# Second block's mixers: two jobs run earlier, output products spread over the last four steps, output units in another order

## What is computed

```python
def token_mixer(h, w_in, f_bias, cmp_pos, cmp_w1, cmp_w2, w_out, cos, sin):
    proj = h @ w_in
    ...
    o_nsa = nsa_mixer(apply_rope(heads(parts['nsa_q'], NSA_HEADS), cos, sin), ...)
    o_fox = fox_mixer(heads(parts['fox_q'], FOX_HEADS), ..., parts['fox_f'], f_bias)
    o_moba = moba_mixer(apply_rope(heads(parts['moba_q'], MOBA_HEADS), cos, sin), ...)
    return jnp.concatenate([o_nsa, o_fox, o_moba], axis=-1) @ w_out
```

## Time and profile before

| what | us |
|---|---|
| runs of the kernel | 1490.35, 1493.84, 1501.74 (median 1493.84) |
| the profiled execution | 1497.93 |
| its span, first to last instruction | 1496.1 |
| TensorE busy | 1454.9 (97% of the span) |
| VectorE busy | 1149.2 (77%) |
| ScalarE busy | 784.7 (52%) |
| DMA engines, mean share | 57.6% by the main queue |
| granted TensorE clock, mean | 0.989 |

### The profile page before, as it was taken

The page is one execution under the profiler, slowest core; times in us unless marked ns, Lnnn a source line. Parts: engine busy times, 40 slices in busy tenths (PEclk is TensorE's granted clock), DMA queues, the critical chain, the costliest instruction groups (busy, mean ns, idle before and its releaser), DMA issues. The chain is left out here.

```text
span 1496.1 us, 20923 instructions
## 1 busy us (share of the span) xinstructions
PE 1454.9 (97%) x8376; PEld 1250.0 (84%) x8376; DVE 1149.2 (77%) x1607; ACT 784.7 (52%) x1115; POOL 26.3 (2%) x31
## 2 busy tenths in 40 slices
PE   8997999999999999999999999999999999999997
PEld 6885888998788888788798888888888787888886
DVE  6797778898779877676678987789877675787653
ACT  7546555764555534656465542655535564565541
POOL 0021000000000000000000000000000000000000
PEclk9999999999999999999999999999999998999999
DMA  8123377988468787433357769478686341466550
...
DMA packets 57152, 327.19 MB, mean 219 GB/s; under 512 B 6608, under 2 KB 7120, under 8 KB 27600
## 3 DMA queue, kind: packets, MB, share of 16 engines
q1 hardware_dynamic: 55440, 322.76, 57.6%
...
## 5 line engine op out<-in xcount | busy, mean ns | idle before, releaser
L335 DVE TENSOR_TENSOR wlo<-raw,whi 128x2048 fp32r<-128x2048 f32 (+2 forms) x236 | 533.5, 2264 | 88.3 <-ACT whi L328 87.3
L328 ACT ACTIVATE whi<-raw 128x2048 fp32r<-128x2048 f32 (+2 forms) x236 | 445.9, 1895 | 133.9 <-PE ps L1603 98.2
L1356 PE MATMUL ps<-hreg_r,whi 128*128 128x512 f32 x1504 | 359.4, 391 | 0.7 <-DVE mix L1539 0.4
L1356 PEld LDWEIGHTS ps<-hreg_r,whi 128*128 128x128 f32 x1504 | 276.6, 188 | 54.8 <-DVE mix L1539 0.6
L370 DVE CUSTOM_DVE_ANT_0 adaw<-adaw,crow,colp 128x1024 f32<-128x1024 f32 x144 | 182.9, 1280 | 37.8 <-DMA adaw<-in_wada 37.6
L1365 PEld LDWEIGHTS ps<-hreg_r,wlo 128*128 128x128 f32 x1504 | 192.6, 191 | 7.0
L1365 PE MATMUL ps<-hreg_r,wlo 128*128 128x256 f32 x1504 | 195.6, 283 | 0.0
L1533 ACT ACTIVATE mix<-ps 128x512 f32<-128x512 f32 x93 | 55.6, 598 | 219.5 <-PE ps L1365 214.1
L1595 PE MATMUL ps<-whi,ireg_r 128*128 128x512 f32 x416 | 130.3, 394 | 3.5 <-ACT ireg_r L1490 3.5
L1599 PE MATMUL ps<-wlo,ireg_r 128*128 128x512 f32 x416 | 128.7, 391 | 0.0
L1603 PE MATMUL ps<-whi,ireg_r 128*128 128x512 f32 x416 | 128.5, 390 | 0.0
(11 more groups left out here) (415 smaller groups left out, 1883.6 us busy)
## 6 DMA issues: line engine op xcount, KB each, us to landing
...
```

Of the source, the lines that this page charges most:

```text
L328: act.activation(self.whi[:, m, 0:width], self.raw[:, n % NRAW, 0:width], ACT.Copy).then_inc(*self.A.done("hi", n))
L335: dve.tensor_tensor(self.wlo[:, m, 0:width], self.raw[:, n % NRAW, 0:width], self.whi[:, m, 0:width].bitcast(F32), ALU.subtract).then_inc( ...
L1356: pe.matmul(self.ps[:, b, :], self.whi[:, m, c:c + 128], self.hboth[:, kt], start=kt == 0, stop=False)
```

## The change

`JOBS` gives each position p the job that runs there: fox's jobs 8 and 9 come fifth and sixth, 4 to 7 seventh to tenth. Semaphores are now named by position. In step order:

- Both pairs of D's heads are turned in step 3 (before, one in step 3 and one in step 4); projection E's second half is copied by ScalarE instead of VectorE.
- The mixed slices kt 4 and 5 (fox) and 6 and 7 (moba) are turned in pairs for all 256 tokens (`turn_pair`, `mixed_pair`), the first pair in step 8. `out` takes parts: six matmuls with kt 4 and 5 stand ahead of `values(8)` and of `values(10)`, and the slices 0 to 3 of tokens 0 follow in the last step, one product on each side of `values(11)`.
- The two compressed products follow each other in step 10; E's heads are turned behind `values(8)`.
- On ScalarE `hidden(0)` and `hidden(1)` stand ahead of the splits that they followed, and the splits of the output units come one place earlier or more. On VectorE the split of unit n0+16 stands ahead of the compressed keys' copies, the next one follows at once, the rope stands behind `maxima(9)`, and `emit` of jobs 4 to 7 releases by its third operation.
- The output units are used and loaded in the order (0, 0), (0, 1), (512, 1), (512, 0) of columns and half.

The diff, cut to its core; the rest renames g to p and defines `turn_pair`, `mixed_pair` and `paired_cols`:

```diff
@@ -58,6 +58,7 @@
 
 
 SPARSE = range(4, 12)
+JOBS = [0, 1, 2, 3, 8, 9, 4, 5, 6, 7, 10, 11]
 
 
 def slot_of(e):
...
-        order.extend([(("w_out2", l), c, h, UW) for h in range(2) for c in (0, 512)])
+        order.extend([(("w_out2", l), c, h, UW) for c, h in ((0, 0), (0, 1), (512, 1), (512, 0))])
         ffn(l, 1)
     return order
 
...
@@ -2377,33 +2384,27 @@
                 mm = pe.matmul(o, self.ahi[:, kv, kt, :], wl, start=False, stop=kt == 15)
             mm.then_inc(*P.done("unit", n))
...
 
-        def out(c, kts, t, free=None):
-
-            if free is not None:
-                pe.wait_ge(*free)
+        def out(c, kts, t, start=False, stop=False):
+
             bank, tk = ps[:, 6 * (1 - t) + c, :], slice(128 * t, 128 * t + 128)
+            n = UNIT[("w_out2", l), 512 * c, kts[0] // 4]
+            m = n % NSPL
+            if t == 0:
+                pe.wait_ge(*A("hi", n))
             for kt in kts:
-                n, i = UNIT[("w_out2", l), 512 * c, kt // 4], kt % 4
-                m = n % NSPL
-                wh = self.whi[:, m, 512 * i:512 * i + 512]
-                if i == 0:
-                    pe.wait_ge(*A("hhi", (st, "o"), kt, t))
-                    pe.wait_ge(*V("hlo", (st, "o"), kt, t))
-                if t == 0 and i == 0:
-                    pe.wait_ge(*A("hi", n))
-                pe.matmul(bank, self.hhi[:, kt, tk], wh, start=kt == 0, stop=False)
+                wh = self.whi[:, m, 512 * (kt % 4):512 * (kt % 4) + 512]
+                pe.matmul(bank, self.hhi[:, kt, tk], wh, start=start and kt == kts[0], stop=False)
                 pe.matmul(bank, self.hlo[:, kt, tk], wh, start=False, stop=False)
             if t == 0:
                 pe.wait_ge(*V("lo", n))
             for kt in kts:
-                i = kt % 4
-                wl = self.wlo[:, m, 512 * i:512 * i + 512]
-                mm = pe.matmul(bank, self.hhi[:, kt, tk], wl, start=False, stop=kt == 7)
+                wl = self.wlo[:, m, 512 * (kt % 4):512 * (kt % 4) + 512]
+                mm = pe.matmul(bank, self.hhi[:, kt, tk], wl, start=False, stop=stop and kt == kts[-1])
             if t == 1:
                 mm.then_inc(*P.done("unit", n))
-            elif kts[-1] == 7:
+                P.at["pj", (st, "o"), c, 1] = P.n
+            elif stop:
                 mm.then_inc(*P.done("pj", (st, "o"), c, 0))
-            P.at["pj", (st, "o"), c, 1] = P.n
 
...
             tr.then_inc(*P.done("zz", st, kv))
 
-        def turn_mix(a, z, t, b):
-            for k in range(a, z):
-                tr = pe.transpose(banks4(b)[:, k - a], self.mix[:, t, 128 * k:128 * k + 128], ident)
-            tr.then_inc(*P.done("mT", st, a, t))
-
-        def scores(g):
-            r = g % 2
-            if g >= 2:
-                pe.wait_ge(*A("pc", st, g - 2))
-                pe.wait_ge(*V("pc", st, g - 2))
...
@@ -2538,18 +2545,19 @@
         scores(3)
         chunk("F", 0, 1, V("pj", st, "D"))
         turned_probs(2)
-        chunk("F", 1, 0)
-        values(2)
         pe.wait_ge(*V("zz", st, 1))
         turn_heads("D", 0)
+        chunk("F", 1, 0)
+        pe.wait_ge(*V("turn", st, "D", 0))
+        turn_heads("D", 1)
+        values(2)
 
         scores(4)
         chunk("F", 1, 1)
         turned_probs(3)
         compress(0, 0, A("pj", st, "F"))
         values(3)
-        pe.wait_ge(*V("turn", st, "D", 0))
-        turn_heads("D", 1)
+        pe.wait_ge(*A("turn", st, "D", 1))
 
         scores(5)
         compress(0, 1)
@@ -2562,7 +2570,6 @@
         turned_probs(5)
         chunk("E", 0, 0, A("hg", st, 0))
         values(5)
-        pe.wait_ge(*A("turn", st, "D", 1))
         pe.wait_ge(*A("hg", st, 1))
         for kv in range(2):
             for k in range(2):
@@ -2594,60 +2601,73 @@
         scores(8)
         chunk("E", 1, 1)
         turned_probs(7)
+        pe.wait_ge(*A("pj", st, "E"))
+        pe.wait_ge(*V("em", st, 5))
+        turn_pair(4, 6)
         values(7)
-
 
         scores(9)
         turned_probs(8)
-        pe.wait_ge(*V("rope", st, 2332))
-        pe.wait_ge(*V("Sc", st))
-        turn_heads("E", 0)
+        pe.wait_ge(*A("hhi", (st, "o"), 4))
+        pe.wait_ge(*V("hlo", (st, "o"), 4))
+        out(0, (4, 5), 0, start=True)
         values(8)
-
-        def compressed(t):
-            pe.matmul(ps[:, 5, :], v["PC"][:, t, :], v["VC"].rearrange("p h d -> p (h d)"), start=True, stop=True)\
-                .then_inc(*P.done("oc", st, t))
-
-        pe.wait_ge(*V("turn", st, "E", 0))
-        scores(10)
-        turn_heads("E", 1)
-        turned_probs(9)
-        pe.wait_ge(*A("turn", st, "E", 1))
         pe.wait_ge(*V("cp", st))
         for t in range(2):
             tr = pe.transpose(ps[:, 5, 128 * t:128 * t + 128], v["Sc"][:, t].rearrange("p g j c -> p (g j c)"), ident)
         tr.then_inc(*P.done("PC", st))
+        pe.wait_ge(*V("rope", st, 2332))
+        for k in range(2):
+            for t in range(2):
+                c = MIXC["E"][0] + 256 * k + 128
+                tr = pe.transpose(banks4(7)[:, 2 * k + t], pj[:, t, c:c + 128], ident)
+        tr.then_inc(*P.done("turn", st, "E", 1))
+        pe.wait_ge(*A("PC", st))
+        turn_heads("E", 0)
+
+        def compressed(t, b):
+            pe.matmul(ps[:, b, :], v["PC"][:, t, :], v["VC"].rearrange("p h d -> p (h d)"), start=True, stop=True)\
+                .then_inc(*P.done("oc", st, t))
+
+        pe.wait_ge(*V("turn", st, "E", 0))
+        scores(10)
+        turned_probs(9)
+        compressed(0, 5)
+        pe.wait_ge(*A("turn", st, "E", 1))
+        compressed(1, 7)
         values(9)
-        pe.wait_ge(*A("PC", st))
-        compressed(0)
 
         scores(11)
+        pe.wait_ge(*V("em", st, 9))
+        pe.wait_ge(*V("oc", st, 1))
+        turn_first(0)
         turned_probs(10)
-        pe.wait_ge(*V("oc", st, 0))
-        compressed(1)
+        out(1, (4, 5), 0, start=True)
         values(10)
-        pe.wait_ge(*V("oc", st, 1))
-        turn_mix(0, 4, 0, 5)
-        turn_mix(0, 4, 1, 0)
+
         turned_probs(11)
-
-
-        out(0, range(4), 0, A("pj", st, "E"))
+        pe.wait_ge(*A("hhi", (st, "o"), 0, 0))
+        pe.wait_ge(*V("hlo", (st, "o"), 0, 0))
+        out(0, range(4), 0)
+        turn_first(1)
         values(11)
-        out(1, range(4), 0, V("pj", st, "E"))
+        pe.wait_ge(*A("hhi", (st, "o"), 0, 1))
+        pe.wait_ge(*V("hlo", (st, "o"), 0, 1))
+        out(1, range(4), 0)
         pe.wait_ge(*V("em", st, 11))
-        turn_mix(4, 8, 0, 5)
-        turn_mix(4, 8, 1, 2)
-        out(0, range(4), 1)
+        turn_pair(6, 2)
+        out(0, range(4), 1, start=True)
+        pe.wait_ge(*A("hhi", (st, "o"), 6))
+        pe.wait_ge(*V("hlo", (st, "o"), 6))
         for c in range(2):
-            out(c, range(4, 8), 0)
-        out(1, range(4), 1)
-        out(0, range(4, 8), 1)
+            out(c, (6, 7), 0, stop=True)
+        out(0, range(4, 8), 1, stop=True)
+        out(1, range(4, 8), 1, start=True)
         self.norm_pe(pe, AFTER[st], 0)
-        out(1, range(4, 8), 1)
+        out(1, range(4), 1, stop=True)
 
     def mixer_sp(self, sp, l):
-        for n in range(UNIT[("w_in2", l), "A", 0], UNIT[("w_out2", l), 512, 1] + 1):
+        for n in range(UNIT[("w_in2", l), "A", 0], UNIT[("w_out2", l), 512, 0] + 1):
             self.ada_sp(sp, n)
             self.loads_at(sp, n)
 
...
@@ -2731,6 +2756,7 @@
         exps(3)
         probs(2)
         self.ahead_act(act, n0 + 8)
+        turned("D", 1, 5)
         act.wait_ge(*V("A", st))
         act.activation(self.ahi, v["A"], ACT.Copy).then_inc(*A.done("Ah", st))
         chunk("F", 6)
@@ -2740,46 +2766,47 @@
         self.ahead_act(act, n0 + 9)
 
         exps(5)
-        turned("D", 1)
         probs(4)
+        hidden(0)
         self.ahead_act(act, n0 + 10)
-        hidden(0)
         self.ahead_act(act, n0 + 11)
 
         exps(6)
         probs(5)
+        hidden(1)
         self.ahead_act(act, n0 + 12)
-        hidden(1)
 
         exps(7)
         probs(6)
         self.ahead_act(act, n0 + 13)
         chunk("E", 6)
+        self.ahead_act(act, n0 + 14)
 
         exps(8)
+        probs(7)
         act.wait_ge(*V("cm", st))
         act.activation(v["S16"], v["S16"], ACT.Exp, scale=0.125).then_inc(*A.done("ce", st))
-        probs(7)
-        self.ahead_act(act, n0 + 14)
+        act.wait_ge(*P("pj", st, "E", 1))
+        act.activation(pj[:, 1, 2332:2844], ps[:, 7, :], ACT.Copy).then_inc(*A.done("pj", st, "E", 1))
+        mixed_pair(4, 6)
 
         probs(8)
         exps(9)
-
-        turned("E", 1)
-        probs(9)
+        self.ahead_act(act, n0 + 15)
         act.wait_ge(*P("PC", st))
         act.activation(v["PC"].rearrange("p t c -> p (t c)"), ps[:, 5, 0:256], ACT.Copy).then_inc(*A.done("PC", st))
+        turned("E", 1, 7)
+
+        probs(9)
         exps(10)
 
+        mixed(0)
         probs(10)
         exps(11)
-        mixed(0, 4, 0, 5)
-        mixed(0, 4, 1, 0)
+        self.ahead_act(act, n0 + 16)
```

(55 more changed lines are left out.)

128 lines of the change are left out of this document (77 added, 51 removed).

## The result

The change made the kernel slower: 1519.11 us, median of four executions (1512.33 to 1524.26), against 1497.26 us for the kernel before, run beside it. The ratio is 1.0129, with a 95% interval of 1.0096 to 1.0162. A second run of the same pair gave 1.0126 (1.0106 to 1.0146): 1517.8 against 1497.5 us by the medians, and 19.3 us more by the means. The forecast was 1505.5 us with a range that ended at 1513, so the size was missed. The ratios are estimated over executions and aren't the quotients of the medians: the two differ by up to 0.2% (1.0129 and 1.0146 in the first run).

The account below looks back on a forecast made before the run. TensorE bounds the mixers, losing time to idling and ungranted clock. Per mixer, 8.4 us new waits less 2.85 removed is +5.55; two mixers +11.1, clock +0.8, on 1493.84 make 1505.7, say 1505.5 us; range 1493 to 1513.

Parts of the forecast that it names:

- `compress(1,1)`: Step 6: the compressor product waits for a split now behind the GELU on ScalarE, 0.9 us a mixer (0.5 to 1.1).
- compressed keys: Compressed scores wait for copies now behind VectorE's split of unit n0+16, 0.65 us a mixer (0.3 to 1.0).
- `values(8)`: Values wait for `emit(7)`, now behind the rope on VectorE: 2.9 us a mixer (2.6 to 3.3) where 1.25 stood.
- E's heads: `scores(10)` waits for the copy of E's turned heads, now turned behind `values(8)`: 0.9 us a mixer (0.7 to 1.2).
- `values(9)`: Values wait for VectorE's split, maxima, probabilities and `emit(8)`: 1.2 us a mixer (0.8 to 1.5).
- small ones: PC's copy behind a split, `emit(9)` ahead of `turn_first(0)`, lower half ahead of the second output product: 0.6 us a mixer.
- into the next stage: Norm behind the mixer: TensorE waits for the diagonal and then the turned tiles, 1.25 us a mixer (0.5 to 2).
- the clock's term: Both mixers: five or six stretches of 3.41 us at half clock in all where five were, +0.8 us.
- the second fall of the kernel before: Clock fall in step 8, said to have no fox in front but a 1.25 us wait; used against regained clock.
- rival C: Clock lost: fox's rows in steps 4 and 5 and the 2.9 us wait add two low stretches a mixer; 1512 us, chance 0.18.
- B: Clock regained in both mixers, waits as worked out: -7.9 us of clock, 1497 us, chance 0.12.
- D: Output matmuls cover `emit(7)` and clock is regained; new waits under 6.8 us a mixer, 1486 us were they 3; chance 0.15.

Follow-up runs that it names:

- the filled wait: Changed kernel with 12 unread matmuls of 512 columns put into TensorE's wait ahead of `values(8)`: 1514.5 us; with the bias rows widened too, 1512.7 us.
- fox128: Fox's bias rows contracted over 128 rows (127 of them zeros) instead of one: changed kernel 1513.7 us; kernel before, ratio 0.9980 and 0.9983.
- the emits first: Kernel before with VectorE's `emit(6)` to `emit(9)` ahead of the maxima and probabilities that stood in front: ratio 0.9968.
- the kernel before with two short waits: Kernel before with `hidden(0)` ahead of ScalarE's split and VectorE's split ahead of the compressed keys' copies: ratio 1.0043.
- the mended places: Changed kernel with VectorE's and ScalarE's order turned in four places: 1498.5 us, 1.0001; `emit(7)` first alone 1.0053, other three 1.0029, two of these 1.0044.

## Why the prediction was wrong

**The waits were right, one by one.** For a mixer, forecast and measured at full clock in the list of waits: `compress(1,1)` 0.9 and 0.91; compressed keys 0.65 and 0.94; `values(8)` 2.9 and 2.8; E's heads 0.9 and 0.85; `values(9)` 1.2 and 1.21, visible in the two kernels with the filled wait; small ones 0.6 and 0.2; into the next stage 1.25 and, at the norm's line, 0.79 and 0.74. The measured ones sum to 8.4 us, as the forecast ones did. Less the 2.85 us that were removed it is 5.55 us a mixer, 11.1 us in all. The mixers' length less 1.2 each says 9.0 us (310.5 less 301.5), and the norms behind them took 2.3 us more: 11.3 us by another way, as far as the net price of 1.2 holds. In the profile of the kernel after itself the wait ahead of `values(9)` isn't there: TensorE, at half its clock, came too late to wait. In its second profile, where the last mixer has one low stretch there instead of three, the wait is back (1.2 us).

The chain at `values(8)` shows that term in full. VectorE and TensorE in the kernel after, in order of time:

```profile
718.16 0.82 PE L2466 MATMUL ps<-cst,ireg 128*128 128x128 f32 x6
719.75 0.61 PE L2402 MATMUL ps<-wlo,hreg_r 128*128 128x512 f32 x2
719.83 0.68 DVE L2843 TENSOR_REDUCE an<-ps 128x2 f32<-128x512 f32 x1
720.65 0.29 DVE L2300 TENSOR_TENSOR rs<-ireg,cosT 128x128 f32<-128x128 f32 x1
721.80 0.28 DVE L2306 TENSOR_TENSOR ireg<-rs 128x128 f32<-128x128 f32 x1
722.65 0.42 DVE L2877 TENSOR_TENSOR mix<-ireg,mix 128x256 f32<-128x256 f32 x1
723.13 0.43 PE L2480 MATMUL ps<-ireg 128*128 128x64 f32 x2 [2.77 <-DVE mix L2877]
```

TensorE has turned the probabilities by 718.7 and has its six output matmuls behind it at 720.36. VectorE is at the maxima until 720.6, then at the rope until 722.0, then at `emit(7)` until 723.07. The rope, which stood ahead of TensorE's arrival in the earlier trace rows, is 1.4 of the 2.8 us; the six output matmuls are over by the time that it begins.

**The step that failed is the clock's term.** "I take five or six low stretches in all where five were: +0.8 us." There are 8 to 12 in the profiles of the kernel after, and the mean clock of its executions, 0.982 against 0.990 of the kernel before beside it, says that this is no chance of a profile. A stretch of 3.41 us at half the clock lowers the mean over 1516 us by 0.5 x 3.41 / 1516 = 0.0011, so 0.008 are seven stretches more. At the net price of 1.2 us they are 8.4 us where +0.8 stood. Fitted within each kernel over all undisturbed executions on record, 0.001 of mean clock goes with 1.2 us, which makes it 9.6. With 11.1 us of waits that is 19.5 to 20.7 us; the second run measured 19.3 us by the means. The interval of its ratio is 6 us wide, so this closes the sum without proving either part to the microsecond. None of the signs of being wrong that the prediction named was a clock that falls further.

A part of the missed time was the base: the forecast stood on a median of 1493.84 us, and the kernel before took 1497.26 us beside the result, 3.4 us more. The rest of the miss, 10.2 us, is what the clock's term lacks (7.6 to 8.8) and the spread of four executions.

The prediction weighed fox's rows and the long wait and let them cancel against fox's leaving step 8. They don't cancel. Three low stretches stand behind the wait ahead of `values(8)` in three of the four mixers profiled of the kernel after (one in the fourth, at 1278.8 of its second profile), and none directly behind it when it is filled. One stands behind fox's rows in their new place in two of these four, in five of the twelve mixers profiled with these rows there, and in none of the six with fox128. Two stand in all four behind the wait for the compressed keys' copies, which the prediction had priced at 0.65 us of waiting and no clock. With the wait filled and fox128 the mean clock is back at 0.990, and the ratio at 1.0070 (5.5 to 15.6 us): the waits' 11.1 us lie inside, and so does what is left of them if the clock, 0.002 above that of before, gave back 2 us. The prediction also misread the second fall of the kernel before ("no fox in front"): the bias rows of fox's second job end at 707.5, 4.6 us ahead of the fall at 712.13, with the 1.27 us wait between them. With fox128, the wait still there, that fall is left in one of four mixers; with the emits first, the rows still there, in none of two. So both seem to have a part in it, as far as so few profiles can tell. The prediction also took one stretch for the long wait, in rival C; it was worth three in a row in three of the four mixers. Behind it come values, transposes and scores, small matmuls all; that this is the reason is likely and not shown.

**The rivals.** C came nearest: it had two more low stretches a mixer, from fox's rows and from the 2.9 us wait, 1512 us. Both causes were right, the third one was missing, and by the mean clock it was three to four more a mixer. B (clock regained) and D (the waits covered) fell: the clock was lowest where B had it whole, and the wait for `emit(7)` was 2.8 us. The range's upper end of 1513 held C and nothing beyond it: a third more stretch a mixer would have made it 1515.

**On the pages.** In the kernel after, ScalarE's table load begins at 681.01 and the split behind the GELU at 682.58, 1.57 us later, and `compress(1,1)` waited 0.91 us. The Trainium skill, ScalarE: Activation LUTs, section What ACT_TABLE_LOAD costs, adds a drain of 1.38 us to the load of 1.28 us; the wait by it would have been 2.3 us, and the trace shows the row's value instead. Three low stretches stood behind an idle wait of 2.77 us and none when it was filled. The Trainium skill, TensorE: Matmul & The Clock Gate, section Why this matters for your kernels, asks for no idle gaps between bursts of matmuls; by that rule the filled wait should keep the clock, and the run agrees. The page means gaps above a length that the 2.77 us here don't quite reach, and the falls behind the 0.94 us wait come from one much shorter. The falls behind fox's rows had no gap in front, in the kernel before as in the kernel after, so the rule isn't all of it.

**What stays open.** Why the kernel before with two short waits lost 6.4 us by its medians and 3.2 by its mixers; why a low stretch comes behind the same rows or the same wait in one mixer and not in the next (five of twelve, eight of ten); what in the bias rows does it, since only one row against 128 was tried; and what part of the single gains of the mended places is clock, since runs of one kernel differ by several stretches.
